# S5 front of a hybrid encoder: tables and C powers dealt out anew between GpSimd and VectorE, and the next weights turned ahead of the input products

## The reference, cut to what matters

```python
def s5_direction(u, lam_re, lam_im, log_step, b_re, b_im, c_re, c_im):
    lam_dt = lam * exp(log_step)
    lam_bar = exp(lam_dt)
    b_bar = ((lam_bar - 1.0) / lam)[..., None] * b
    bu = einsum('lbgh,gph->lbgp', u, b_bar)
    h = associative_scan(h[t] = lam_bar * h[t-1] + bu[t])
    return einsum('ghp,lbgp->lbgh', c, h).real

u = x @ w_in
y = y_fw + y_bw + d_skip * u
y = gelu(y)
y = y * sigmoid(y @ w_glu + b_glu)
return y @ w_out
```

## Time and profile before

| what | value |
|---|---|
| median of 3 runs | 2645.22 us (2644.72 to 2647.85) |
| the profiled execution | 2644.07 us |
| its span, first to last instruction | 2642.3 us |
| mean granted TensorE clock | 0.973 |
| TensorE, VectorE, GpSimd busy | 2488.7, 1920.4, 727.2 us |
| S5 block, up to the last gate product | about the first 400 us |

### The profile page before, as it was taken

How to read it: one execution, slowest core, us unless ns; L and a number is a source line. 1 busy time by engine, 2 the same in 40 slices (tenths; PEclk the granted TensorE clock), 3 DMA queues, 4 the chain that set the end, 5 groups by cost and what they waited for, 6 DMA issues and landing times. The chain is left out here.

```text
span 2642.3 us, 39850 instructions
## 1 busy us (share of the span) xinstructions
PE 2488.7 (94%) x12860; PEld 2085.5 (79%) x12860; DVE 1920.4 (73%) x3122; ACT 900.0 (34%) x1455; POOL 727.2 (28%) x557
## 2 busy tenths in 40 slices
PE   7678799999999999999999999998799999999997
PEld 6567687878888878887888888887677888887886
DVE  8879826777877758884667666676586777785887
ACT  3223324243333335523322223223124333333641
POOL 6768810243333310001111111112024333331000
PEclk9888899999999999999999999999899999999999
DMA  4143314056677678722010110100404667667863
GB/s 146 56 118 105 97 56 160 13 150 214 192 222 214 204 264 281 233 102 63 25 41 24 40 32 24 40 24 16 159 8 135 203 207 220 209 200 259 296 207 130
DMA packets 442288, 355.97 MB, mean 135 GB/s; under 512 B 30272, under 2 KB 376512, under 8 KB 438464
## 3 DMA queue, kind: packets, MB, share of 16 engines
q1 hardware_dynamic: 442176, 354.52, 42.9%
HBM read 296.31 MB, written 58.13 MB: 134 GB/s over the span
## 5 line engine op out<-in xcount | busy, mean ns | idle before, releaser
L2514 PE MATMUL ps<-aT_hi,w_hi 128*128 128x512 f32 x624 | 250.7, 402 | 3.8 <-DVE hg_q_raw L2793 2.0
L2464 POOL TENSOR_TENSOR w_lo<-w_raw_plain,w_hi 128x1024 fp32r<-128x1024 f32 x38 | 90.9, 2401 | 575.3 <-ACT w_hi L62 575.3
L2514 PE MATMUL ps<-aT_hi,w_lo 128*128 128x512 f32 x624 | 245.2, 393 | 0.0
L2514 PE MATMUL ps<-aT_lo,w_hi 128*128 128x512 f32 x624 | 243.8, 391 | 0.0
L616 PE MATMUL ps<-aT_hi,hgo_w_sets 128*128 128x512 f32 x640 | 203.0, 393 | 0.0
L616 PE MATMUL ps<-aT_hi,s5o_w_sets 128*128 128x512 f32 x640 | 202.7, 393 | 0.0
L1284 POOL TENSOR_TENSOR s5o_w_sets_plain<-s5o_w_sets_plain 128x512 f32<-128x512 f32 x80 | 109.9, 1374 | 216.7 <-DMA s5o_w_sets_plain<-in_ffn_w_in_dram 216.7
L1284 POOL TENSOR_TENSOR hgo_w_sets_plain<-hgo_w_sets_plain 128x512 f32<-128x512 f32 x80 | 110.6, 1383 | 212.8 <-DMA hgo_w_sets_plain<-in_ffn_w_in_dram 212.8
L616 PEld LDWEIGHTS ps<-aT_hi,hgo_w_sets 128*128 128x128 f32 x640 | 120.4, 188 | 26.4
L616 PEld LDWEIGHTS ps<-aT_hi,s5o_w_sets 128*128 128x128 f32 x640 | 120.2, 188 | 26.3
L2514 PEld LDWEIGHTS ps<-aT_hi,w_hi 128*128 128x128 f32 x624 | 117.5, 188 | 26.9 <-DVE hg_q_raw L2793 2.4
(11 more groups left out here) (445 smaller groups left out, 6246.9 us busy)
## 6 DMA issues: line engine op xcount, KB each, us to landing
s5o_w_sets_plain<-in_ffn_w_in_dram SPq DMA_DIRECT2D x168, 256.0 KB, 3.2
hgo_w_sets_plain<-in_ffn_w_in_dram SPq DMA_DIRECT2D x168, 256.0 KB, 3.3
w_raw_plain<-in_hg_w_in_dram SPq DMA_DIRECT2D x40, 512.0 KB, 3.9
aT_hi_plain<-in_ffn_w_out_dram SPq DMA_DIRECT2D x64, 256.0 KB, 4.6
s5o_w_sets_plain<-in_ffn_w_in_dram SPq DMA_DIRECT2D x96, 128.0 KB, 2.7
hgo_w_sets_plain<-in_ffn_w_in_dram SPq DMA_DIRECT2D x96, 128.0 KB, 2.8
s5o_hidden<-s5o_home_plain SPq DMA_DIRECT2D x11, 1024.0 KB, 7.0
hgo_hidden<-hgo_home_plain SPq DMA_DIRECT2D x11, 1024.0 KB, 6.8
```

The costliest lines, as they stand in the source:

```text
L2464: g.tensor_tensor(w_lo[b][:, :, :], w_raw[b][:, :, :], w_hi[b][:, :, :].bitcast(F32), ALU.subtract).then_inc(E[f"w_lo_done{b}"], 1)
L2514: ins = t.matmul(ps[:, half, :], w[b][:, kk, :], x[:, kk, cols], start=(kk == 0 and q == 0), stop=(kk == KT - 1 and q == 2))
```

## The change

Eight edits, all in the S5 block:

- VectorE's `tables_to_first_power` (11 steps, after the sine) becomes `tables_to_inverse` (4 steps, after the tanh). The other steps are GpSimd's now (`first_power`, 8 steps), ahead of `later_powers`.
- `make_bl(0)` is VectorE's alone.
- GpSimd waits for `mu` before `split_w(1)`, and makes only the backward C powers of tile 0, ahead of `split_w(2)`.
- The forward C powers of tile 0 are VectorE's, in PSUM, after `scan(0)`; `make_kern(0)` waits for those of tiles 0 and 1.
- TensorE has `start_state(1)` between the two halves of `inputs(2)`; ScalarE's copies follow that order.
- In the loop TensorE has `turn_bl(n + 1)` ahead of `inputs(n + 2)`.
- ScalarE has `place_b(n + 1)`, `keep_min(n + 1)`, `place_c(n + 1)` ahead of `keep_u(n + 2)` and `split_w(n + 3)`, from n = 2 on.
- `turned_diagonal(n)` comes after the first level of `scan(n)`, for n = 1 that of tile 0.

The diff, without most of its unchanged lines and the list of semaphores:

```diff
     LAM_READY = ROWS_READY + 4 + 7
-    FIRST_POWER = LAM_READY + GJ - 1 + 11
-    POW = 18
+    INVERSE = LAM_READY + GJ - 1 + 4
+    EXP, POW = 8, 18
     SCAN = 4 * (2 * LV - 1) + 2 * 4
...
-    def make_bl(e, n, sides=(0, 1), sem="bl", temp=None):
-        link = Steps(S[sem], n and n * BL - BL // 2)
-        for d in sides:
+    def make_bl(e, n):
+        link = Steps(S["bl"], n * BL)
+        for d in range(2):
             half = [P, PR, L, GRP]
...
             pows = [bc(asc[:, q, at, L - 1::-1] if d == 0 else asc[:, q, at, 0:L], 3, half) for q in range(2)]
-            product_steps(link, e, b, pows, [bl[:, q, dps] for q in range(2)],
-                          gen_t[:, :, 0:L, :] if temp is None else temp)
+            product_steps(link, e, b, pows, [bl[:, q, dps] for q in range(2)], gen_t[:, :, 0:L, :])
...
     def make_cl_in_psum(e, n):
-        link = Steps(S["cl_fw"], (n - 1) * CLF)
+        link = Steps(S["cl_fw"], n * CLF)
         for b in range(2):
...
                 if n >= 1:
-                    t.wait_ge(S["bl"], (n + 1) * BL - BL // 2)
+                    t.wait_ge(S["bl"], (n + 1) * BL)
                 if n == 0:
...
                     t.wait_ge(S["kern_rows_done"], n)
-                    t.wait_ge(S["cl_fw"], (n - 1) * CLF)
+                    t.wait_ge(S["cl_fw"], n * CLF)
                 for m in range(4):
                     if n == 0:
-                        t.wait_ge(S["bl" if m < 2 else "bl_bw"], BL // 4 * (m % 2 + 1))
+                        t.wait_ge(S["bl"], BL // 4 * (m + 1))
                     if m >= 2:
...
             def make_kern(n):
-                t.wait_ge(S["cl"], (n + 2) * CLS)
-                t.wait_ge(S["cl_fw"], (n or 1) * CLF if n < KT - 1 else (n - 1) * CLF + CLS)
+                t.wait_ge(S["cl"], (n + 1) * CLS)
+                t.wait_ge(S["cl_fw"], ((n or 1) + 1) * CLF if n < KT - 1 else n * CLF + CLS)
                 if n >= 1:
...
             turn_bl(1)
-            inputs(2, (0, 1))
+            inputs(2, (0,))
             start_state(1)
+            inputs(2, (1,))
             make_kern(0)
...
                 across_chunks(n - 1)
+                if n < KT - 1:
+                    turn_bl(n + 1)
                 if 2 <= n < KT - 2:
                     inputs(n + 2, (0, 1))
-                if n < KT - 1:
-                    turn_bl(n + 1)
...
             def place_c(n):
-                a.wait_ge(S["min_kept"], 4 * (n + 1))
+                a.wait_ge(S["min_kept"], 4 * ((n or 1) + 1))
+                if n == 1:
+                    a.wait_ge(S["cl_fw"], CLF)
                 a.activation(c_turned, c_all[:, 0, :, n * PR:(n + 1) * PR, :], ACT.Copy).then_inc(S["c_placed"], 1)
...
             keep_min(1)
+            place_c(0)
+            keep_u(2, (0,))
+            keep_state(0)
             place_c(1)
-            keep_u(2)
+            keep_u(2, (1,))
             split_w(3)
-            keep_state(0)
             keep_kern_rows(0)
...
                     keep_y(n - 1)
-                if n + 2 < KT:
+                if n == 1:
                     keep_u(n + 2)
-                if n + 3 < KT:
                     split_w(n + 3)
...
                     keep_y(0)
+                if n >= 2 and n + 2 < KT:
+                    keep_u(n + 2)
+                    if n + 3 < KT:
+                        split_w(n + 3)
                 if n == KT - 2:
...
-            def tables_to_first_power():
-                v.wait_ge(S["tab_act"], 4)
-                done(v.tensor_tensor(W["c1"], W["half"], W["half"], ALU.mult))
-                done(v.tensor_scalar(W["c1"], W["c1"], -2.0, None, ALU.mult))
-                done(v.tensor_scalar(W["cos"], W["c1"], 1.0, None, ALU.add))
+            def tables_to_inverse():
+                v.wait_ge(S["tab_act"], 2)
                 done(v.tensor_scalar(W["t"], W["tanh"], -1.0, 1.0, ALU.mult, ALU.add))
                 done(v.reciprocal(W["t"], W["t"]))
-                done(v.scalar_tensor_tensor(W["em"], W["tanh"], 2.0, W["t"], ALU.mult, ALU.mult))
-                done(v.tensor_scalar(W["e"], W["em"], 1.0, None, ALU.add))
                 done(v.memset(asc[:, 0, :, 0], 1.0))
                 done(v.memset(asc[:, 1, :, 0], 0.0))
-                done(v.tensor_tensor(asc[:, 0, :, 1], W["e"], W["cos"], ALU.mult))
-                done(v.tensor_tensor(asc[:, 1, :, 1], W["e"], W["sin"], ALU.mult))
-                assert link.n == FIRST_POWER
+                assert link.n == INVERSE
...
             def tables_to_input_factors():
+                v.wait_ge(S["exp"], EXP)
                 done(v.tensor_tensor(W["m_re"], W["em"], W["cos"], ALU.mult))
...
                 last = halves(False, lambda d: v.wait_ge(S["in_done"], 4 * n + 2 * (d + 1)))
-                if n == KT - 1:
+                if n == 1:
+                    turned_diagonal(0)
+                if n >= 2:
                     turned_diagonal(n)
...
                     last = whole(lv, False, last)
-                if n == 1:
-                    turned_diagonal(0)
-                if 2 <= n < KT - 1:
-                    turned_diagonal(n)
                 for lv in range(LV - 2, 0, -1):
...
                 split_x(n)
-            tables_to_first_power()
+            tables_to_inverse()
             for n in range(4, XT):
...
             v.wait_ge(S["pow"], POW)
-            make_bl(v, 0, (0,))
+            make_bl(v, 0)
             scan_factors()
...
             scan(0)
+            v.wait_ge(S["c_placed"], 1)
+            make_cl_in_psum(v, 0)
             for n in range(1, KT):
                 if n < KT - 1:
-                    v.wait_ge(S["c_placed"], n)
+                    v.wait_ge(S["c_placed"], n + 1)
                     if n >= 2:
...
+            def first_power():
+                link = Steps(S["exp"])
+
+                def done(ins):
+                    ins.then_inc(S["exp"], 1)
+                    g.wait_ge(S["exp"], link.step())
+
+                g.wait_ge(S["tab"], INVERSE)
+                done(g.tensor_tensor(W["em"], W["tanh"], W["t"], ALU.mult))
+                done(g.tensor_scalar(W["em"], W["em"], 2.0, None, ALU.mult))
+                done(g.tensor_scalar(W["e"], W["em"], 1.0, None, ALU.add))
+                g.wait_ge(S["tab_act"], 4)
+                done(g.tensor_tensor(W["c1"], W["half"], W["half"], ALU.mult))
+                done(g.tensor_scalar(W["c1"], W["c1"], -2.0, None, ALU.mult))
+                done(g.tensor_scalar(W["cos"], W["c1"], 1.0, None, ALU.add))
+                done(g.tensor_tensor(asc[:, 0, :, 1], W["e"], W["cos"], ALU.mult))
+                done(g.tensor_tensor(asc[:, 1, :, 1], W["e"], W["sin"], ALU.mult))
+                assert link.n == EXP
+
             split_w(0)
-            g.wait_ge(S["tab"], FIRST_POWER)
+            first_power()
             later_powers()
-            g.wait_ge(S["bar"], BAR)
-            make_bl(g, 0, (1,), "bl_bw", cl[0][:, 0, 0:PR, 0:L, :])
+            g.wait_ge(S["mu"], 1)
             split_w(1)
-            g.wait_ge(S["bl"], BL // 2)
             ins(1)
+            g.wait_ge(S["c_kept"], 8)
+            make_cl(g, 0, 1, S["cl"], 0)
             split_w(2)
-            g.wait_ge(S["mu"], 1)
-            g.wait_ge(S["c_kept"], 8)
-            make_cl(g, 0, 0, S["cl"], 0)
-            make_cl(g, 0, 1, S["cl"], CLS)
             split_w(3)
...
                     g.wait_ge(S["out_done"], n - 1)
-                make_cl(g, n, 1, S["cl"], (n + 1) * CLS)
+                make_cl(g, n, 1, S["cl"], n * CLS)
                 if n == KT - 1:
-                    make_cl(g, n, 0, S["cl_fw"], (n - 1) * CLF)
+                    make_cl(g, n, 0, S["cl_fw"], n * CLF)
                 if n + 1 < KT:
```

More of the change, by code:

```diff
@@ L1407, in s5_gate_block @@
         "x_hi", "x_lo", "b_turned", "b_kept", "c_turned", "c_kept", "w_loaded", "w_hi_done", "w_lo_done", "u_done",
-        "u_kept", "bar", "bl", "bl_bw", "pow", "cl", "b_placed", "kern_done", "kern_rows_kept",
+        "u_kept", "bar", "bl", "pow", "exp", "cl", "b_placed", "kern_done", "kern_rows_kept",
         "kern_rows_done", "kern_out", "toep_placed", "u_out", "u_grouped", "bl_turned", "min_kept", "in_done",
```

## The result

The changed kernel took 2675.5 us (median of 4 runs, 2674.9 to 2677.8), the kernel before 2645.1 beside it: ratio 1.0116 [1.0102, 1.0130], 30.5 us slower. Predicted were 2673 (2661 to 2684). The profiled execution took 2675.2 us against 2644.1.

The account below looks back on a forecast made before the run. TensorE, VectorE and GpSimd were nearly full, none quite; the change closes a ring of 43.8 us a round against 31.67. Sum +28.4 us (28.0 to 30.9): median plus sum 2673.6, profiled plus sum 2672.5; predicted 2673, range 2661 to 2684.

Parts of the forecast that it names:

- The ring: S5 loop: GpSimd's lower weight part, C powers, bl, TensorE's turns, input products, ScalarE's u, w_hi in sequence: 43.8 us a round.
- the signs named: New profile: TensorE waits 8 to 10 us for bl, scans 43 to 44 apart, mu at 47 to 49, scan(1) near 91.
- ScalarE's new order: S5 loop: place_b, keep_min, place_c ahead of keep_u and split_w cost the ring nothing; VectorE's 1.46 us waits go.
- The wait of VectorE: S5 loop: with the early diagonal VectorE may wait about 3 us for the kernel product, hidden in the 43.8 us round.
- The x splits: Front: four VectorE steps remain and need only the tanh, so splits resume about 3 us sooner (bounds 0 to 3.5).
- mu: Front: with GpSimd waiting, VectorE finishes mu at 47.7 us, some 19 us sooner; upper bound 50.5.
- The entry into the ring: End of the front: inputs(4) starts at 154.3 us, behind the turn of bl of tile 3, just when it did before.
- The whole front gain is gone: End of the front: inputs(4) starts just when it did before, as GpSimd pays for its rest.
- The tail: S5's end: scan(6) +30.9 us, GpSimd's last C powers +28.0; the end follows GpSimd, scan's end having about 6 us slack.
- VectorE did not pace the loop: Rival: VectorE's own work sets S5 rounds of 30.2 us; −15 to −25 us, about 2625; chance 0.08.
- GpSimd was not quicker: Rival: in S5's loop GpSimd's 24.54 us falls to 20 while VectorE idles; +15 us, 2660; chance 0.06.
- The lower clock: Rival: low clock lasts into S5's input products, 1.7 us a round, and x splits gain nothing; +36.5, 2682; chance 0.09.

Follow-up runs that it names:

- e2: The kernel before with the loop edits alone (TensorE's and ScalarE's new order, early diagonal), old front kept: 2666.9 us, ratio 1.0087.
- e1: The changed kernel with TensorE's and ScalarE's loop order as before; new front and early diagonal kept: 2643.6 us, ratio 0.9994.
- e6: The changed kernel with GpSimd's split of a weight one round later and SyncE's loads of weights 6 and 7 to match: 2638.6 us, ratio 0.9974.
- e4: The changed kernel with GpSimd's bl products from tile 3 on cut to a quarter of their elements: 2648.3 us, ratio 1.0015.
- e3: The changed kernel with TensorE's loop order alone as before, ScalarE's new order kept: 2658.3 us, ratio 1.0056.

## Why the prediction was right, and where its sizes were off

**The ring** was the cause, shown from both sides: the loop edits alone close it (e2), their removal opens it (e1), and so does a later split with the edits kept (e6). Its length was predicted as 43.8 us and is 43.96 and 44.13. Its terms, from 169.44: GpSimd from the end of the split (171.81) to the end of bl (196.12) 24.3 (24.54); the turns until the first input product at 199.66 3.5 (3.8); the input products until 211.7 12.0 (11.25); back to the end of the next split at 215.76 4.1 (4.08). Three closed rounds give scan(6) its delay: 3 × 43.4 from 173.12 to 303.40, against 3 × 31.2 from 176.11 to 269.68 before. Of the signs named, scans 43 to 44 us apart came as 43.6, 43.9 and 42.8, scan(1) near 91 at 93.7. TensorE's waits for bl were 7.3 to 7.7 us and not 8 to 10: the prediction let only VectorE wait for the kernel product, but TensorE itself waited 4.1 us a round for the C powers ahead of it. The turns would not have been shorter at full clock, as the lower end of the prediction's range for the round, 42.6, has it: in e4, where 8 of them take 1.09 us, their stage lasts 3.51 us with ScalarE's copies.

**ScalarE's new order** was priced at nothing "for the ring". In the closed ring nothing speaks against that, but e3 shows it is no free move: with TensorE's order of before it costs 13.8 us by a ring of its own, of 36 to 37 us, which the prediction did not see. It is hidden under the longer one.

**The wait of VectorE** for the kernel product, about 3 us, was 3.19 at 181.90, and hidden.

**The x splits** came 1.9 us sooner (17.43 against 19.36), not 3. The four steps did "need only the tanh", but had no price: the first of them, 64 elements, took 2.30 us at 14.03, while GpSimd's split of weight 0 ran from 13.93 to 16.27. A step of that kind and size had taken 0.20 before, in the timeline of VectorE there:

```profile
16.50 0.20 DVE L2077 TENSOR_SCALAR s_cl<-s_cl 128x64 f32<-128x64 f32 x1
```

The Trainium skill ("SBUF — State Buffer", "Who interferes with whom") names tensor_scalar among the operations that can take the pair of ports shared with GpSimd, if their operands meet certain conditions, and says that the later issued one then blocks fully; the row agrees, as it ends at 16.33, right behind GpSimd's at 16.27.

**mu** was predicted at 47.7 and came at 48.3.

**The entry into the ring** was predicted at 154.3 and came at 156.49. The largest part arose in inputs(2): its first half was put at 5.6 us and took 7.7 (77.73 until ScalarE's copy of u at 85.45). The row at 79.60 shows why: these products came 0.43 us apart, not 0.23, behind a wait of 6.75 us, and the granted clock was 0.50 (1.2 GHz) from 77.7 to 81.7 us and 1.00 (2.4 GHz) from 82 to 85. The start of start_state(1) slipped from 83.9 to 86.7 by it, GpSimd's next split from 95.2 to 97.75, and the turn of tile 2 from 122.2 to 124.58.

**"The whole front gain is gone"** was too mild, and that inputs(4) stands where it did is partly chance. With the early diagonal the front is worth 0 (e1: 0.9994 [0.9981, 1.0007]). In the company of the loop edits it is a loss of 8.6 us (e2), since those let the old front enter at 148.10. The prediction gave the early diagonal no price of its own; at the turn of tile 2 it is worth 7.7 us (118.18 instead of 125.86), and the new front, with bl at 124.5, takes nearly all of it back.

**The tail.** The sum had +28.4, measured are +30.5 (+31.2 between the profiled spans). The term that was mis-sized is the entry. GpSimd's last C powers started at 311.96 instead of 281.51, that is +30.45 where the sum had +28.0, and 2.2 of these 2.45 us are the entry's. (A small term there is misread: the kernel's products and those within chunks are 212.04 − 209.12 = 2.92 by the earlier trace rows, not 3.1.) The slack of the scan's end was put at about 6 us and was 3.85: VectorE's y part was done at 325.11 before and needed by the gate product at 328.96. Now it is done at 360.17, 35.06 later, so the product at 360.23 waited 2.47 us for it, and the end is 35.06 − 3.85 = 31.2 us late. That adds only 0.8 to GpSimd's delay. The 60 gate products ahead of it started within 13.6 us (from 343.74, granted clock 1.00), where before it had been 15.5 (from 313.28, behind a wait of 3.64, the first eight at 0.50).

**The rivals.** VectorE did not pace the loop, since bl was late in each round. What stood against this rival was the order of GpSimd's queue, the split ahead of the C powers; e6 takes just that away, and the loop is quick again, though it gives −6 and not −20. The rounds are not the reason: from scan(3) at 170.31 to scan(7) at 290.69 e6 needs 30.1 us each. The rival counted such rounds from scan(1) on and so had scan(3) at about 152, while the forecast's own sum reaches inputs(4) only at 154.3. GpSimd was not quicker (24.3 us against 24.54), although VectorE waited 7 to 10 us a round. The lower clock was there, 0.79 from 200 to 300 us where it had been 0.86, but cost under 1 us a round in the input products.

## What to carry to other kernels

Before a consumer is turned ahead of independent work in one queue, follow the in-order queue of each engine that feeds it until the path comes back or ends: if it comes back, its round is the sum of all its parts without any overlap, however idle every engine looks. Making a part of such a ring faster shortens it (e4), and moving one step that has slack a round later opens it; here one split moved turned +30 us into −6. And an engine that is made to rest so that another runs undisturbed must have that time free in its own queue: 19 us won on VectorE were worth nothing, as GpSimd's split of weight 2 came at 75.34 instead of 64.52 and tile 2's bl at 124.5 instead of 116.5. And small edits that only serve a larger one want a price of their own: the early diagonal was worth 7 us at scan(2) with the old front.

## What the runs showed of the hardware that was not expected

A 64-element step of VectorE with a single input took 2.30 us instead of 0.20 beside one GpSimd instruction of 2.34 us. The levels of the scan's factors, small steps with two inputs, were 4.5 times as long beside a busy GpSimd (3.52 against 0.79 us). And TensorE came out of its waits at the lower clock: after 7.65 us of waiting it was granted 0.50 from 196.1 to 201.1 us, and 1.00 from 201.5 to 210. 16 turns took 3.83 us there, where 8 took 1.09 in e4 without a wait. The cost beyond the wait itself was 0.8 us, in the input products; the turns lost nothing, as they are paced by ScalarE's copies at the full clock.
